# One PSUM bank for all products and one for all row inverses in a forgetting-attention kernel

## The reference

```python
c = jnp.cumsum(lf, axis=1)                      # log of the forget gates
s = jnp.einsum('bqhd,bkhd->bhqk', q_i, k).astype(jnp.float32) * scale
s = s + (c_i[..., :, None] - c_keys[:, :, None, :])
s = jnp.where(kpos[None, :] <= qpos[:, None], s, -jnp.inf)
p = jax.nn.softmax(s, axis=-1).astype(v.dtype)
out = jnp.einsum('bhqk,bkhd->bqhd', p, v)
# later: concat(out, memory attention) * silu(gate), then @ w_out
```

## Time and profile before

| | |
|---|---|
| time, median of 3 runs | 4038.05 us (4037.72 to 4039.57) |
| profiled execution | 4038.05 us, of which the span on the engines is 4036.6 us |
| TensorE busy | 3542.2 us, 88% of the span |
| VectorE busy | 1882.9 us, 47% |
| ScalarE busy | 1315.8 us, 33% |
| GpSimd busy | 336.6 us, 8% |
| prompt attention of layer 0 | 1762 to 2495 us of the span, 8 heads |

### The profile page before, as it was taken

The page is one execution under the profiler, slowest core; times in us unless marked ns, Lnnn a source line. Parts: engine busy times, 40 slices in busy tenths (PEclk is TensorE's granted clock), DMA queues, the critical chain, the costliest instruction groups (busy, mean ns, idle before and its releaser), DMA issues. The chain is left out here.

```text
span 4036.6 us, 56501 instructions
## 1 busy us (share of the span) xinstructions
PE 3542.2 (88%) x19825; PEld 3080.7 (76%) x19825; DVE 1882.9 (47%) x3378; ACT 1315.8 (33%) x2438; POOL 336.6 (8%) x549
## 2 busy tenths in 40 slices
PE   5699997799999999968888886899599599996999
PEld 4599996588888887757777775688599577774787
DVE  4311222356666654547766775432311245474432
ACT  1211222245545543445555553111211254310111
POOL 0131000001111110101011110000000000131000
PEclk8799998899999999979999998899799799997899
DMA  4333432567777764322223322332322244565332
GB/s 136 102 99 94 132 96 87 131 191 241 236 230 226 241 196 129 123 83 86 84 106 108 101 89 74 117 110 79 92 96 96 89 123 131 161 213 165 111 109 80
DMA packets 385337, 523.94 MB, mean 130 GB/s; under 512 B 52855, under 2 KB 275064, under 8 KB 380495
## 3 DMA queue, kind: packets, MB, share of 16 engines
q1 hardware_dynamic: 317255, 398.72, 31.6%
q0 software_dynamic: 30624, 93.22, 7.0%
q10 hardware_dynamic: 37248, 29.37, 2.4%
HBM read 388.83 MB, written 132.74 MB: 129 GB/s over the span
## 5 line engine op out<-in xcount | busy, mean ns | idle before, releaser
L382 ACT ACTIVATE z_st_p<-bank 128x352 f32<-128x352 f32 (+3 forms) x325 | 168.1, 518 | 759.2 <-PE bank L365 758.4
L1330 PE MATMUL bank<-w_hi_o,b_hi_o 128*128 128x512 f32 x816 | 328.9, 403 | 71.4 <-DVE w_lo_o L1372 71.4
L338 DVE CAST w_hi_p<-w_raw_p 128x1024 fp32r<-128x1024 f32 (+1 forms) x130 | 89.2, 686 | 540.8 <-PE bank L365 510.1
L365 PE MATMUL bank<-h00hi,w_hi_p 128*128 128x352 f32 x984 | 320.2, 325 | 11.2 <-DVE w_lo_p L340 7.7
L1331 PE MATMUL bank<-w_hi_o,b_lo_o 128*128 128x512 f32 x816 | 324.6, 398 | 0.0
L1332 PE MATMUL bank<-w_lo_o,b_hi_o 128*128 128x512 f32 x816 | 324.4, 398 | 0.0
L365 PE MATMUL bank<-h00hi,w_lo_p 128*128 128x352 f32 x984 | 317.1, 322 | 0.0
L365 PE MATMUL bank<-h00lo,w_hi_p 128*128 128x352 f32 x984 | 317.0, 322 | 0.0
L365 PE MATMUL bank<-h01hi,w_hi_p 128*128 128x512 f32 x656 | 270.5, 412 | 8.9 <-DVE w_lo_p L340 8.9
L365 PE MATMUL bank<-h01lo,w_hi_p 128*128 128x512 f32 x656 | 259.1, 395 | 0.0
L365 PE MATMUL bank<-h01hi,w_lo_p 128*128 128x512 f32 x656 | 258.4, 394 | 0.0
(11 more groups left out here) (361 smaller groups left out, 8652.7 us busy)
## 6 DMA issues: line engine op xcount, KB each, us to landing
z<-z_st_p SPq DMA_DIRECT2D x128, 512.0 KB, 2.8
k_raw_sf<-in_cache_fox_k SPq DMA_DIRECT2D x128, 512.0 KB, 4.3
v_raw_sf<-in_cache_fox_v POOLq DMA_DIRECT2D x128, 512.0 KB, 4.4
w_raw_p<-in_fox_w_in SPq DMA_DIRECT2D x80, 512.0 KB, 5.2
b_raw_o<-bT SPq DMA_DIRECT2D x32, 768.0 KB, 7.5
w_raw_p<-in_pool_w_in SPq DMA_DIRECT2D x48, 512.0 KB, 4.8
out<-tok_fa ACTq DMA_DIRECT2D x64, 256.0 KB, 2.3
w_raw_o<-in_w_out ACTq DMA_DIRECT2D x24, 512.0 KB, 3.9
```

Of the source, the lines that this page charges most:

```text
L365: last = nc.tensor.matmul(out, wt[:, u, k, :], h[:, k, at0:at0 + width], start=(m == 0), stop=(m == MM - 1))
L382: nc.scalar.activation(z_st[0:rows, t % 2, at0:at0 + width], banks[n % 2][0:rows, 0:width], func).then_inc(z_read, 1)
L1330: nc.tensor.matmul(out, bh, w_hi[:, k, cols], start=(k == 0), stop=False)
```

## The change

All products go to the left half of bank 6, all spread inverses to the left half of bank 7. Since the products of block j now use the bank that block j-1 used, the wait at their start is for `mix` of block j-1. The spreading matmul of block j moves: it was behind the last product of the block, in the last part of step 5+2j; it now stands at the head of that step, before its scores, behind waits for `dg` of block j and for `mix` of block j-1. VectorE's two reads follow the new banks. Its order, and those of ScalarE, GpSimd and SP, stay as they were.

```diff
--- before.py
+++ after.py
@@ -490,7 +490,7 @@
     NP = first[NQ]
     TG = 8
     S_BANKS, T_BANKS = banks[0:4], banks[4:6]
-    OUT = [(banks[6 + n][:, 0:QW], banks[6 + n][:, QW:2 * QW]) for n in range(2)]
+    O_BANK, R_BANK = banks[6], banks[7]
     NB = 4
     LAG = 2
     with ExitStack() as s:
@@ -605,6 +605,12 @@
                     last.then_inc(kvt, 1)
                 pe.wait_ge(lo_d, 2 * h + 3)
                 for qs, qt, product, _ in steps():
+                    if product is not None and product[1] == 1:
+                        j = product[0]
+                        pe.wait_ge(dg_d, NCH * h + j + 1)
+                        pe.wait_ge(mix_d, NCH * h + j + 2)
+                        nc.tensor.matmul(R_BANK[:, 0:QW], ones[:, :],
+                                         dg[:, :, :].rearrange("p a n -> p (a n)"), start=True, stop=True).then_inc(r_done, 1)
                     n_parts = max(1, parts(qs, qt))
                     for p in range(n_parts):
                         if qs is not None and p < pieces[qs]:
@@ -629,21 +635,18 @@
                             shared = range(n_keys * at // of, n_keys * (at + 1) // of) if p >= late else ()
                             for n in (n_keys * half + x for x in shared):
                                 if n == 0:
-                                    pe.wait_ge(mix_d, NCH * h + j + 1)
+                                    pe.wait_ge(mix_d, NCH * h + j + 2)
                                     pe.wait_ge(tl_d, NP * h + first[QB * (j + 1)] + 2)
                                 if n % 4 == 0:
                                     pe.wait_ge(vlo, 4 * h + n // 4 + 2)
                                 c0 = max(0, n - QB * j) * P
-                                out = OUT[j % 2][0][:, c0:QW]
+                                out = O_BANK[:, c0:QW]
                                 ph, pl = pT_hi[:, j % 2, n, c0:QW], pT_lo[:, j % 2, n, c0:QW]
                                 nc.tensor.matmul(out, v_hi[:, n, :], ph, start=(n == 0), stop=False)
                                 nc.tensor.matmul(out, v_lo[:, n, :], ph, start=False, stop=False)
                                 last = nc.tensor.matmul(out, v_hi[:, n, :], pl, start=False, stop=(n == QB * (j + 1) - 1))
                                 if n == QB * (j + 1) - 1:
                                     last.then_inc(o_done, 1)
-                                    pe.wait_ge(dg_d, NCH * h + j + 1)
-                                    nc.tensor.matmul(OUT[j % 2][1], ones[:, :],
-                                                     dg[:, :, :].rearrange("p a n -> p (a n)"), start=True, stop=True).then_inc(r_done, 1)
                         if qt is not None and p < pieces[qt]:
                             g = first[qt] + p
                             if p == 0:
@@ -716,11 +719,11 @@
 
                         dve.wait_ge(r_done, NCH * h + j + 2)
                         dve.wait_ge(g_in[j % 2], 16 * (NCH // 2 * h + j // 2 + 1))
-                        nc.vector.tensor_tensor(gate[:, j % 2, :], gate[:, j % 2, :], OUT[j % 2][1], ALU.mult).then_inc(gr_d, 1)
+                        nc.vector.tensor_tensor(gate[:, j % 2, :], gate[:, j % 2, :], R_BANK[:, 0:QW], ALU.mult).then_inc(gr_d, 1)
                         dve.wait_ge(gr_d, NCH * h + j + 1)
                         dve.wait_ge(o_done, NCH * h + j + 3)
                         dve.wait_ge(stored, NCH * h + j + 1)
-                        nc.vector.tensor_tensor(mix[:, j % 2, :], gate[:, j % 2, :], OUT[j % 2][0], ALU.mult).then_inc(mix_d, 1)
+                        nc.vector.tensor_tensor(mix[:, j % 2, :], gate[:, j % 2, :], O_BANK[:, 0:QW], ALU.mult).then_inc(mix_d, 1)
                     if qs is not None and qs % 4 == 0:
 
                         jn, w = qs // 4, 512 * (qs // 4 + 1)
```

## The result

The changed kernel takes 4074.4 us (median of 4 runs, 4069.1 to 4075.5) against 4037.9 us (4037.6 to 4039.6) before: ratio 1.0087, 95% interval 1.0069 to 1.0104. It is slower by 36.5 us, where 21.1 were predicted, and lies above the range (4070). The profiled execution took 4075.3 us with a span of 4073.8, 37.2 more than the span before.

What follows compares the result with a forecast made beforehand. The prediction took the ring and TensorE's own queue to bound the attention stage by turns. Per head 1.16+0.48+1.29-0.25 = 2.68 us for seven heads, 2.3 for the last: 21.1 us on 4038.05, forecast 4059.1 us, range 4047 to 4070.

Steps and rivals of the forecast that it cites:

- a gap of 1.40 brings no fall now: Argument against a clock fall: TensorE's 1.40 us gap ahead of block 7's products brought none before the change.
- The rival that the clock falls: Clock drops behind the longer gap at block 7's products in half the heads: 12 us more, 4071; chance 0.12.
- Sum of the waits: All stalls and the boundary gain over eight heads: 2.68 us a head for seven, 2.3 the last, 21.1 us together.
- Block 1, +1.16: Spread(1), ahead of the scores, waits for dg(1), made after mix(0)'s store is issued: 1.16 us a head.
- Block 3, +0.48: Products wait 1.31 us for mix; a 0.43 us gap takes part, and pT_lo starts 0.48 us later.
- Blocks 2, 4, 5, 6, nothing: Waits at blocks 2, 4 and 6 end in TensorE's gaps at transposes; block 5 has none: cost 0.
- Block 7, +1.29: Tail of the head: first product waits for mix(6) and starts 1.29 us later, with nothing behind taking it back.
- Boundary, -0.25: Between heads: VectorE no longer waits for the last spread, so next scores get back 0.25 us of the delay.
- Not slower: Rival: early spread frees VectorE before gate(7) and gaps cover every new wait: 4035.7 us; chance 0.08.
- the ring: Repeating chain: row maximum on VectorE, exponential, pT_hi on ScalarE, pT_lo on VectorE, next maximum; alternates with TensorE's queue as limit.

Runs made afterwards that it cites:

- e2: Kernel before the change, two product banks kept, inverses in the other bank's right half, spread moved, gate a step earlier: 4038.0 us.
- e8: e2 with GpSimd making dg of the next block ahead of the store: 4026.8 us, ratio 0.9972 to the kernel before the change.
- e9: Changed kernel with 39 extra matmuls a head, results unused, in the new gaps at blocks 1 and 7, all waits kept: 4056.0 us.
- e3: Changed kernel with GpSimd making dg of the next block ahead of its wait for mix and the store: 4057.6 us.
- e5: Kernel before the change, with block 7's products alone also waiting for mix(6), though they write another bank: 4059.5 us.
- e11: Changed kernel, one product bank, with dg of the next block ahead of the store and gate a step earlier: 4042.0 us.
- e10: Changed kernel with dg of the next block ahead of the store and 20 extra matmuls ahead of block 7's wait: 4054.5 us.
- e6: Changed kernel with gate(6) and mix(6) moved ahead of the last pT_lo in VectorE's order: 4060.6 us.
- e7: e6 with GpSimd also making dg of the next block ahead of the store: 4055.7 us.

## Why the prediction was wrong

Its direction was right, and so was the sum of the waits that it predicted from, though by some luck: block 3 was priced 0.3 us too high, the tail 0.2 too low and the boundary's gain 0.15 too high, and these nearly cancel. The step that failed is the one that set the clock aside: "Against: a gap of 1.40 brings no fall now". That sentence is true, and e2 and e8 bear it out in 16 more heads. But the change makes a gap of 2.9 us, and the reason speaks of 1.40. Behind 2.9 us the clock fell in 23 of 32 tails, behind 1.9 in 13 of 24. The rival that the clock falls was given 0.12, and 12 us on top of the waits; it is what happened, and with 18.0 us (after less e9).

Point by point:

- **Sum of the waits.** Predicted 21.1 us; e9, which has them all and no falls from mix(0) to mix(7), shows 20.8 in the stage and 19.5 in the medians. In heads of after that keep their clock the sum is 1.22 up to mix(6), 0.77 at the tail and 0.63 at the boundary: 2.62 us against 2.68.
- **Block 1, +1.16.** 7.43 - 6.31 = 1.12. The cause, dg(1) behind the store of mix(0), is shown by e3, which takes it away and has 6.35.
- **Block 3, +0.48.** 9.77 instead of 9.59: 0.18. More of the wait lay in gaps than I had read.
- **Blocks 2, 4, 5, 6, nothing.** 9.15, 12.32, 13.47, 11.94 instead of 9.16, 12.32, 13.53, 11.95. Right.
- **Block 7, +1.29.** The product starts 0.24 us after mix(6) ends (0.27 in the head shown), where I took the 0.05 of another handover; so the wait adds 1.48 (1.51 in the head shown; e5 by itself: 1.45). The pause of 0.55 ahead of mix(6) stayed in every kernel in which gate(6) is right in front of it, and went in e11.
- **Boundary, -0.25.** Tail and boundary together are 0.77 + 0.63 = 1.40 where 1.04 was predicted: against the 1.51 of the wait, some 0.1 came back. In e5 nothing did.
- **The clock at the tail.** The rival's price was right for its place: tails of after sum to 68.0 us, eight at 7.03 would be 56.2, so 11.8 against the 12 it named. That it comes so close is luck: it reckoned with four falls of 2.9 us, and there were seven, six of them of 1.5.
- **The clock at block 1.** Not in the prediction at all, not in the rival either: 520.6 - 8 x 64.1 = 7.8 us. The two gaps of 0.8 to 1.46 and 0.81 with some 1.1 us of work between them were priced as waits only.
- **Not slower.** The early spread did not free VectorE, since gate(7) still waits 3.8 us for it. That an early *gate* gains 1.9 us a head is what e11 against e3 shows, and the prediction did not see; it took gate as fixed behind pT_lo.

"TensorE: Matmul & The Clock Gate", "A second HAM failure mode: psum-queue depth-cycling", in the Trainium skill, tells of small idles between matmul groups that make the clock swing. With the change the runs agree with it in kind: the clock falls at block 1 between groups of products and scores, in 15 of 18 heads that show a gap of 1.46 us and most of them a second one of 0.8 to 1.0. The Trainium skill's "PSUM — Partial Sum Buffer", "Summary: rules for kernel authors", has a reader of PSUM and a running matmul use different banks. Keeping to it with one bank of products takes waits: e8 and e11 differ by the bank and its waits alone, and by 15 us.

What stays open: in which heads the clock falls, since the same gaps in the same kernel bring a fall in some and not in others; a gap of 1.33 us ahead of block 6's products, seen in the second head of every kernel with one bank but e11, that never brought one, where 1.46 at block 1 did; whether one of 0.8 us at block 1 could bring one without a fall shortly before; why the handover from mix(6) takes 0.24 us and that from mix(0) 0.06; the pause of 0.55; the spread of e10's times. The rest of the span, whose code is the same, differs by 1.6 us between the two profiled executions, which is a measure of what a single span can tell.

## What to carry to other kernels

Two accumulators that take turns let TensorE start the next block while another engine reads the last one; with one, each block's first product waits for that reader, and the wait costs where no gap of TensorE covers it, above all at the end of a loop. Price a new gap on TensorE twice: its length, and the clock behind it. Here a wait of 1.5 us that widened a gap from 1.4 to 2.9 cost another 1.5 us in seven of ten heads, so compare the gap after the change, not the one before, with what the trace shows as harmless. And look for instructions that stand in the ring only by their order (gate in front of mix, dg behind the store): moved to where their engine waits anyway, they took back some 30 of the 36.5 us with one bank (e11), and made two banks 11 us faster than before (e8).

## What the hardware did that I had not expected

- A fall costs 1.5 us in most tails (8.55 against 7.03, 9.21 against 7.71) and 2.6 in some (9.68, 10.28), and it can start with the work behind the gap: in after's second head the first rows after 2.92 us of standing are at full speed, and the row of 0.28 us becomes 0.41 some 0.8 us later. In the dearest tails it starts earlier, inside the gap: in e5's second head the clock is 0.50 before the first product, which lasts 0.55 us instead of 0.35, and the tail takes 10.28.
- Useless work made the kernel faster: 39 more matmuls a head, 17 to 18 us less (e9 against after).
- Some kernels vary more than others: e5's six runs differ by up to 18.3 us and e10's five by 18.9, where the kernel before differs by 8.7 us in the eleven runs beside e5 (4034.9 to 4043.6) and by 7.4 in the fifteen beside e10 (4033.8 to 4041.2). Falls that come in some heads only don't explain it alone: e3 has them too, and its five runs differ by 3.0 us.
- VectorE's result reached TensorE after 0.05 to 0.06 us at most places, and after 0.23 to 0.27 at block 7 wherever mix(6) came last, with a gap of 0.25 us (e9) as with one of 2.9. Where pT_lo came last at the same product (before, e2, e6, e7, e8) it was 0.05 to 0.06.
